# Next group's first two evictions ahead of y's high parts in ScalarE's sequence of an SSD stage

## The reference

```python
zxbcdt = h @ w_in                                  # z, x, B, C and dt
xbc = silu(causal_dwconv(xbc, conv_w, conv_b))     # width 4, depthwise
dt = softplus(dt_raw + dt_bias);  a_head = -exp(a_log)
a_cs = cumsum(dt * a_head)                         # within a chunk
lmat = exp(where(tri, seg(a_cs), -inf))
y_diag = einsum(cb, lmat, x * dt);  cb = C . B
states = einsum(B, exp(a_cs[-1] - a_cs), x * dt)   # scanned over chunks
y_off = einsum(C, prev, exp(a_cs))
y = (y_diag + y_off + xs * d_skip) * silu(z)
return rms_norm(y, norm_w) @ w_out
```

## Time and profile before

| | |
|---|---|
| median of 3 runs | 1354.79 us |
| the profiled execution | 1355.58 us, its span 1353.8 us |
| TensorE busy | 1333.6 us (99%) |
| VectorE busy | 777.9 us (57%) |
| ScalarE busy | 570.6 us (42%) |
| GpSimd busy | 24.4 us (2%) |
| HBM read and written | 132.51 MB and 2.16 MB |
| SSD groups 1 to 7 | from about 76 to 358 us of the span |

### The profile page before, as it was taken

One profiled execution on the slowest core, in us unless ns is written; L12 is line 12 of the kernel. 1 busy time (PEld: TensorE's weight loads), 2 busy tenths in 40 slices (PEclk: granted clock), 3 DMA queues, 4 the chain that ended last, 5 costly groups with the idle time before them and its releaser, 6 DMA issues.

```text
span 1353.8 us, 15929 instructions
## 1 busy us (share of the span) xinstructions
PE 1333.6 (99%) x6474; PEld 1115.1 (82%) x6474; DVE 777.9 (57%) x1139; ACT 570.6 (42%) x875; POOL 24.4 (2%) x28
## 2 busy tenths in 40 slices
PE   8999999999999999999999999999999999999998
PEld 6878787877888988888888888888898888888886
DVE  4878778787624666666642266545466656664223
ACT  6666555666324534333331163222453333333112
POOL 0000000000000000000000000000000000000000
PEclk9999999999999999999999999999999999999999
DMA  4532234332242233333343313333223333334331
GB/s 148 162 109 70 89 107 125 110 112 74 79 140 63 63 109 109 94 96 103 97 126 102 115 47 96 104 96 112 91 63 109 108 95 93 94 103 130 93 109 62
DMA packets 181773, 135.70 MB, mean 100 GB/s; under 512 B 5645, under 2 KB 169893, under 8 KB 180677
## 3 DMA queue, kind: packets, MB, share of 16 engines
q1 hardware_dynamic: 181653, 134.62, 33.0%
q10 hardware_dynamic: 48, 0.07, 0.0%
HBM read 132.51 MB, written 2.16 MB: 99 GB/s over the span
## 4 chain that ended last, share of the span: by engine, by line
PE 83%; DVE 7%; ACT 5%; issue 2%; DMA 2%; SPq 0%; DVEq 0%
PE bank L850 17%; PE bank L851 17%; PE bank L852 17%; PE bank L911 9%; PE bank L913 9%; PE bank L912 9%; DMA w_raw<-in_ssd_w_in 2%; DVE mask L637 2%; DVE feat L709 1%; ACT w_hi L355 1%; ACT e_row L428 1%; DVE w_lo L586 1%; PE bank L888 1%; DVE feat L703 1%; ACT L413 1%
## 5 line engine op out<-in xcount | busy, mean ns | idle before, releaser
L850 PE MATMUL bank<-h_hi,w_hi 128*128 128x512 f32 (+1 forms) x1352 | 513.7, 380 | 0.0
L852 PE MATMUL bank<-h_lo,w_hi 128*128 128x512 f32 (+1 forms) x1352 | 511.0, 378 | 0.0
L851 PE MATMUL bank<-h_hi,w_lo 128*128 128x512 f32 (+1 forms) x1352 | 510.8, 378 | 0.0
L586 DVE TENSOR_TENSOR w_lo<-w_raw,w_hi 128x1024 fp32r<-128x1024 f32 x228 | 278.4, 1224 | 356.6 <-ACT w_hi L355 356.5
L355 ACT ACTIVATE w_hi<-w_raw 128x1024 fp32r<-128x1024 f32 x228 | 238.2, 1052 | 203.2 <-PE bank L913 172.8
L852 PEld LDWEIGHTS bank<-h_lo,w_hi 128*128 128x128 f32 x1352 | 254.3, 188 | 47.2
L850 PEld LDWEIGHTS bank<-h_hi,w_hi 128*128 128x128 f32 x1352 | 254.4, 188 | 46.5
L851 PEld LDWEIGHTS bank<-h_hi,w_lo 128*128 128x128 f32 x1352 | 254.4, 188 | 46.3
L911 PE MATMUL bank<-w_hi,hid_hi 128*128 128x512 f32 x416 | 162.4, 390 | 0.0
L913 PE MATMUL bank<-w_hi,hid_lo 128*128 128x512 f32 x416 | 161.9, 389 | 0.0
L912 PE MATMUL bank<-w_lo,hid_hi 128*128 128x512 f32 x416 | 161.8, 389 | 0.0
(11 more groups left out here) (146 smaller groups left out, 944.4 us busy)
## 6 DMA issues: line engine op xcount, KB each, us to landing
w_raw<-in_ffn_w_up SPq DMA_DIRECT2D x88, 512.0 KB, 3.8
w_raw<-in_ssd_w_in SPq DMA_DIRECT2D x48, 512.0 KB, 4.0
w_raw<-in_ffn_w_down SPq DMA_DIRECT2D x44, 512.0 KB, 3.5
w_raw<-in_sc_w_in SPq DMA_DIRECT2D x24, 512.0 KB, 3.7
acs_b<-acs_dram SPq DMA_DIRECT2D x8, 1024.0 KB, 6.2
w_raw<-in_ssd_w_out SPq DMA_DIRECT2D x16, 512.0 KB, 3.5
w_raw<-in_sc_w_out SPq DMA_DIRECT2D x8, 512.0 KB, 3.6
x_tok<-in_x SPq DMA_DIRECT2D x4, 512.0 KB, 4.9
```

The costliest lines, as they stand in the source:

```text
L586: nc.vector.tensor_tensor(w_lo[slot(u)][:], w_raw[:, u % 2, :], w_hi[slot(u)][:].bitcast(F32), ALU.subtract).then_inc(w_lo_done, 1)
L850: nc.tensor.matmul(dst, wh, xh, start=start, stop=False)
L851: nc.tensor.matmul(dst, wl, xh, start=False, stop=False)
L852: return nc.tensor.matmul(dst, wh, xl, start=False, stop=stop)
```

## The change

In ScalarE's sequence of the SSD stage:

- the evictions of the next group's B and C leave the head of the loop for every group but the first. B's goes behind the exponentials of the next mask, ahead of y's high parts; C's goes behind both y tiles, ahead of the row exponentials. Each takes with it the split of weights that `conv_in` ends with;
- the silu of B and of C stand in front of the eviction of x0 in every group. Before, this was so in group 0 alone.

```diff
             for g in range(GROUPS):
-                conv_in(g, 0, CONV_T - 2 * GROUPS + g)
-                conv_in(g, 1, CONV_T - GROUPS + g)
-                if g:
-                    conv_in(g, 2, g * XG)
-                    conv_out(g, 0)
-                    conv_out(g, 1)
-                else:
-                    conv_out(g, 0)
-                    conv_out(g, 1)
-                    conv_in(g, 2, g * XG)
+                if g == 0:
+                    conv_in(g, 0, CONV_T - 2 * GROUPS + g)
+                    conv_in(g, 1, CONV_T - GROUPS + g)
+                conv_out(g, 0)
+                conv_out(g, 1)
+                conv_in(g, 2, g * XG)
+                if g == 0:
                     exps(g)
                     exps_row(g)
                 conv_in(g, 3, g * XG + 1)
...
                 if g < GROUPS - 1:
                     exps(g + 1)
+                    conv_in(g + 1, 0, CONV_T - 2 * GROUPS + g + 1)
                 for j in range(XG):
...
                 if g < GROUPS - 1:
+                    conv_in(g + 1, 1, CONV_T - GROUPS + g + 1)
                     exps_row(g + 1)
```

## The result

The changed kernel takes 1345.43 us (median of 6 runs, 1345.36 to 1345.69), the kernel before 1354.70 us (6 runs, 1354.41 to 1355.74): ratio 0.9931, 95% interval 0.9918 to 0.9944. That is 9.3 us less; forecast were 1345.5 us and 9.3 us. In the series of the experiments the kernel before had medians of 1355.2 to 1355.3 us, so a difference of half a microsecond between two series of runs means nothing.

The account below looks back on a forecast made before the run. TensorE, busy 1333.6 of 1353.8 us, was taken to bound the kernel. Removing its wait for the silu, 8.2 + 7 x 0.16 = 9.3 us off the 1354.79 us median, gave 1345.5 us, range 1343.8 to 1348.5.

Parts of the forecast that it names:

- The term: TensorE's wait at L1003 for the silu of C goes in seven groups: 8.2 us idle plus 7 x 0.16, 9.3 us.
- the unpriced restart: Small restarts on TensorE that go with the waits, given no size; the range was widened to 1343.8 us for them.
- Eviction of B: ScalarE: evicting B ahead of y idles 0.6 us waiting for B's end; y_hi(0) starts at about 195.25, 2.6 us later.
- Eviction of C, row exponentials: ScalarE: C's eviction and split last until 200.7, the row exponentials until 202.85 instead of 199.4, at no price.
- VectorE: VectorE's queue is freed earlier: low half of x1's weights done at 199.1, C's taps at 203.7, z0's split at 204.9.
- the first rival: The wait moves to VectorE's chain, as GpSimd's adds block y_lo and x1's split: 1350.3 us, chance 0.08.
- the prediction's worst case: VectorE held up by both GpSimd adds: x1's split ends at 201.3, silu C at 206.7, still 2.5 us ahead of L1003.
- Silu first: ScalarE: silu of C ends at 205.3 instead of 210.5, 3.9 us before TensorE can take it at 209.2.
- What is late next: VectorE's path to L1021 is tightest, with 0.9 us ahead of the split and 1.1 behind; nothing becomes a wait.
- Nothing is won: At L1003 something equally late takes the silu's place on TensorE: time stays 1354.8 us, chance 0.05.
- Slower: TensorE stops at x1's matmuls for late low-half weights, a loss from 205.0 on: 1360 us, chance 0.03.
- the two paths named: Silu of C to the C·B matmuls, 3.9 us to spare; VectorE's chain through xdd to the states, 2.0 in sum.

Follow-up runs that it names:

- narrow_adds: Changed kernel, but GpSimd adds only one column of each square to the total: 1345.66 us, ratio 0.9929.
- silu_first_only: Kernel before with the silu of B and C ahead of x0's eviction in every group, evictions of B and C unmoved: 1348.44 us, ratio 0.995.
- spare_2: Changed kernel with two spare ScalarE exponentials ahead of the row exponentials in groups 1 to 7: 1348.48 us, ratio 0.995.

## Why the prediction was right

*The term.* Forecast were 1.33 us per group, the mean idle time and 0.16 us for the modelled end. Measured: 41.16 - 39.75 = 1.41, or 9.9 us for seven. The 0.08 us more are at L1003 itself. Behind the wait its matmuls took 1.16 us, now 1.05 (the longest single one 377 ns before, 275 after). That is the restart which the prediction left unpriced and had widened its range for. The spans of the two traces differ by 10.1 us: 9.9 in the groups and 0.3 ahead of the first group, whose L1003 started at 45.15 and now L1002 at 44.87. The medians differ by 9.3 only, because the profiled execution of before lay 0.9 us over its median (1354.70) and that of after at its own. Of these 0.9 us, 0.3 are those ahead of the first group; where the other 0.6 lie stays open, as there is one trace of the kernel before. So the mechanism and the size per group are right, but that the forecast meets the medians to a tenth of a microsecond is luck: the unpriced restart (some 0.6 us in all) and the 0.3 us ahead of the first group happen to be as much as the 0.9 us by which the profiled execution lay over its median.

*Eviction of B.* The forecast is right to 0.1 us: ScalarE idles 0.71 us (0.6 forecast), starting 0.03 us after B's end, y_hi(0) at 190.64, which is 195.1 in the old turn (195.25 forecast).

*Eviction of C, row exponentials.* They end at 198.24, in old times 202.7 (202.85).

*VectorE.* The forecast had x1's split done at 199.1, or 201.3 at worst. Measured 200.6: the adds of GpSimd came in, as the first rival had them, with the first y_lo undisturbed. narrow_adds shows that they are the cause, and that all of it stood under cover. So the mechanism of the rival was at work, but not its loss: it cost no time, as the prediction's worst case had it.

*Silu first.* Forecast 3.9 us of cover, measured 3.4 (201.21 to 204.65), since the silu of C waits 0.40 us for C's taps, which x1's long split had held back. With the adds cut the wait is gone and the cover is 3.96 us.

*What is late next.* The prediction named VectorE's chain to the states, with 0.9 us idle ahead of the split and 1.1 behind. Measured 0.59 us and 1.16 (xdd ends at 216.55, L1020 starts at 217.71). The 0.9 is the idle time of the kernel before carried over; the prediction's own times (the mask product's end at about 217, the split 1.38 us earlier than 219.14) give less, 0.8. It is the tighter path, as the spare instructions showed.

*The rivals.* "Nothing is won" fell with L1003's start to start of 0.23 us. "Slower" had its threshold at x1's weights at 205.0, measured 200.6. Where a slower outcome does lie the last experiments show: with three spare instructions, some 4.5 us of ScalarE per group, the changed kernel is slower than the one before (1358.95 us), and there the two paths named and the transposes of x1 decide, not x1's weights.

What the prediction did not see is that the change is larger than its effect needs. From the rows it had, the eviction of B alone could have been worked out to take the whole wait away, because x0's eviction then waits for TensorE; that came only with the experiments.

## What to carry to other kernels

Once a wait is gone, moving more gains nothing: work out for each part of a reordering when the late value is there with that part alone, and count the rest as cover. Give the cover of each path in microseconds; one or two instructions of spare work of known length then test these numbers in a run. The list of waits counts each wait of TensorE too short by what the modelled end of the matmul ahead hides (0.39 less 0.23 us here), and a short one may be missing from it: 0.31 us stood there in none of seven groups of silu_first_only and in one of seven of spare_2. Compare starts.

## What the runs showed of the hardware

A stall of TensorE that the list puts at 1.17 us (8.2 in 7) cost 1.41 per group: 0.16 us of it lie under the modelled end of the matmul ahead, and the C·B matmuls behind it took 1.16 us instead of 1.05, at a granted clock of 1.00 in both kernels. Behind a gap of 0.31 us the states took 1.53 us instead of 1.46. Why the first matmul behind a stall is longer, no run shows. And a VectorE instruction with two inputs in SBUF stands still while GpSimd adds from SBUF: w_lo 2.31 us instead of 1.22, y_lo 1.32 instead of 0.75, and both back at 1.22 and 0.75 with the adds cut to one column. The Trainium skill has this in "SBUF — State Buffer", section "Who interferes with whom"; the runs agree, for SCALAR_TENSOR_TENSOR as well.
